# Scatter and weight transposes moved ahead of the wait for gate and up weights, in passes of four experts

## What is computed

```
gate   = weights of the top 8 of 64 experts per token        # 256 tokens in all
act    = silu(einsum('td,edf->tef', t, w_gate)) * einsum('td,edf->tef', t, w_up)
routed = einsum('tef,efd->td', act * gate[:, :, None], w_down)
```

## Time and profile before

| | |
|---|---|
| median of 3 runs | 1548.76 us (1547.97 to 1551.95) |
| profiled execution | 1552.18 us |
| its span, first to last instruction | 1550.5 us |
| TensorE busy | 1422.1 us, 92% of the span |
| transfers | 507.48 MB, mean 327 GB/s |
| mean granted clock of TensorE | 0.970 of full |

### The profile page before, as it was taken

How to read it: one execution, slowest core, us unless ns; L and a number is a source line. 1 busy time by engine, 2 the same in 40 slices (tenths; PEclk the granted TensorE clock), 3 DMA queues, 4 the chain that set the end, 5 groups by cost and what they waited for, 6 DMA issues and landing times. The chain is left out here.

```text
span 1550.5 us, 28139 instructions
## 1 busy us (share of the span) xinstructions
PE 1422.1 (92%) x11994; PEld 741.8 (48%) x11995; DVE 425.4 (27%) x1070; ACT 259.5 (17%) x485; POOL 118.0 (8%) x349
## 2 busy tenths in 40 slices
PE   3999979999999989999969998989998999999996
PEld 2675656434434434444446666564443444344442
DVE  2291774311111111111135537460111111111112
ACT  1313213211101111111113231141110111111110
POOL 2610630000000000000000026000000000000000
PEclk8899999999999999999989999989999999999999
DMA  6854950699999999999845678119999999999994
GB/s 245 281 181 174 362 193 8 284 405 421 420 419 406 410 421 404 420 418 421 359 162 174 237 267 309 52 59 405 421 421 420 421 405 410 419 413 421 414 420 189
DMA packets 114116, 507.48 MB, mean 327 GB/s; under 512 B 14880, under 2 KB 20796, under 8 KB 64572
## 3 DMA queue, kind: packets, MB, share of 16 engines
q1 hardware_dynamic: 113372, 504.43, 81.3%
q0 software_dynamic: 384, 1.05, 0.2%
q10 hardware_dynamic: 224, 0.06, 0.0%
HBM read 503.41 MB, written 2.10 MB: 326 GB/s over the span
## 5 line engine op out<-in xcount | busy, mean ns | idle before, releaser
L971 PE MATMUL ps<-ring,h 128*32 128x512 f32 x2720 | 373.3, 598 | 23.7 <-DMA ring<-in_exp_w_up 15.0
L971 PEld LDWEIGHTS ps<-ring,h 128*32 128x32 f32 x2720 | 109.5, 111 | 245.6 <-issue 245.5
L990 PE MATMUL ps<-ring,work 128*32 128x512 f32 x1360 | 199.6, 598 | 3.1 <-DVE store L1636 1.6
L971 PE MATMUL ps<-store,h 128*32 128x512 f32 x608 | 189.5, 616 | 10.8 <-issue 7.2
L997 PE MATMUL ps<-store,work 128*128 128x512 f32 x416 | 192.4, 605 | 1.6 <-DVE store L1644 1.6
L957 PEld LDWEIGHTS ps<-tm,work 128*128 128x128 bf16 x2496 | 144.4, 98 | 44.3 <-issue 43.1
L957 PE MATMUL ps<-tm,work 128*128 128x128 bf16 x2496 | 156.9, 219 | 0.3
L1634 DVE TENSOR_TENSOR work<-work,ps 128x256 f32<-128x256 f32 x52 | 21.9, 422 | 408.5 <-ACT work L1299 408.5
L997 PEld LDWEIGHTS ps<-store,work 128*128 128x128 f32 x416 | 74.7, 189 | 120.0 <-issue 116.5
L1636 DVE COPY store<-ps 128x512 f32<-128x512 f32 x52 | 36.0, 692 | 328.9 <-PE ps L990 328.9
L681 PE MATMUL ps<-ring,store 128*128 128x512 f32 (+1 forms) x256 | 100.7, 552 | 0.0
(11 more groups left out here) (296 smaller groups left out, 1222.3 us busy)
## 6 DMA issues: line engine op xcount, KB each, us to landing
ring<-in_exp_w_gate SPq DMA_DIRECT2D x102, 1024.0 KB, 14.7
ring<-in_exp_w_up SPq DMA_DIRECT2D x102, 1024.0 KB, 17.1
ring<-in_exp_w_down SPq DMA_DIRECT2D x102, 1024.0 KB, 15.4
ring<-in_w_ada SPq DMA_DIRECT2D x28, 2048.0 KB, 10.3
store<-in_exp_w_gate SPq DMA_DIRECT2D x26, 1024.0 KB, 15.2
store<-in_exp_w_up SPq DMA_DIRECT2D x26, 1024.0 KB, 17.7
work<-in_exp_w_down SPq DMA_DIRECT2D x26, 1024.0 KB, 15.4
ring<-in_w_in SPq DMA_DIRECT2D x6, 2048.0 KB, 12.5
```

The lines of the kernel that those rows point to most:

```text
L971: last = mm(ps[first:first + TILE, 4, :], X_e[:, b, kt, first:first + TILE], gate_up(slot, kt), start=(kt == 0), stop=(kt == KT - 1))
L990: last = mm(ps[first:first + TILE, 7, :], turn[:, P * j + first:P * j + first + TILE], down(slot, j, half), start=(j == 0), stop=(j == 1))
```

## The change

In a pass of four experts, other than p = 0, the two transposes of routing weights and the scatter of the rows of the pass before are issued ahead of the wait for the gate and up weights. In the other passes nothing moves. No instruction is added or removed, SyncE's, ScalarE's and VectorE's programs stay as they are.

```diff
                 used = [EXPERT_PASS.index(p) + c for c in range(len(PLACED[p]))]
+                late = p > 0 and len(used) == P // TILE
+                if late:
+                    pe.wait_ge(s["S_ready"], p + 1)
+                    turn_weights()
+                    pe.wait_ge(s["Y_kept"], 2 * p)
+                    scatter().then_inc(s["scattered"], 1)
                 for k in used:
                     pe.wait_ge(gate_in[expert_slot(k)], 32 * (k // SLOTS + 1))
                 pe.wait_ge(s["X_kept"], 2 * p + 2)
                 gate_up_pass(q, tiles(p)).then_inc(s["gu_done"], 1)
-                if p:
+                if p and not late:
                     pe.wait_ge(s["Y_kept"], 2 * p)
                     scatter().then_inc(s["scattered"], 1)
-                pe.wait_ge(s["S_ready"], p + 1)
-                turn_weights()
+                if not late:
+                    pe.wait_ge(s["S_ready"], p + 1)
+                    turn_weights()
                 pe.wait_ge(s["act_done"], p + 1)
                 turn_acts().then_inc(s["turned"], 1)
```

## The result

The changed kernel takes 1553.7 us (median of 17 runs, 1549.4 to 1560.39). The kernel before takes 1547.97 us (median of 17 runs, 1544.34 to 1552.51). The ratio is 1.0039, with a 95% interval of 1.0025 to 1.0053; the medians differ by 5.7 us. The forecast was 1556.4, slower, in a range of 1550 to 1560.

What follows compares the result with a forecast made beforehand. TensorE (92% busy) and the transfers (nine tenths in expert passes) were both taken as nearly full. Layer ends of +4.1 and +3.5 sum to 7.6, profiled 1552.18 to 1559.8; the median, 3.4 lower, gives 1556.4 us, range 1550 to 1560.

Steps and rivals of the forecast that it cites:

- the price of a pass: Each changed pass: 4.44 us added ahead of gate_up_pass, 2.68 saved behind, so it ends later by 1.76 - W.
- the clock that falls at p = 16: At p = 16, layer 2: a wait grown to 3.0 us lowers TensorE's clock, so lateness goes from +1.8 to +3.5.
- the cost of the late release: Buffers released 4.44 us late behind p = 11 leave a 2.5 us transfer hole; behind p = 20 another, 2.0.
- W: TensorE's wait ahead of a pass's gate_up_pass in the kernel before, from none at p = 11 to 3.34 us at p = 15.
- What p = 15 gains is not kept: At p = 15, layer 2: the pass ends 0.8 us sooner, but p = 16 still waits for its own weights.
- The rival in which it holds: Clock stays up at p = 16 after a 3.0 us wait; layers end +1.8 and +2.4, 1553.0 us; chance 0.12.
- the floor: Shortest time from issue to landing of up weights on a drained queue: taken as 8.9 us, with 6.8 for the range.
- the second rival: Queue always holds enough (6.8 us to landing); only last passes lose, 0.5 and 1.1 us: 1550.4 us; chance 0.16.
- called p = 6 even: At p = 6, a wait of about 1.66 us was to offset the change within 0.1 us.
- The last passes: At p = 25, the change was to lose 1.11 us in layer 1 and 0.52 in layer 2.
- the faster rival: Waits ahead of p = 25 grow long, so each last pass ends 2.68 us sooner: 1543.4 us; chance 0.07.
- Holes everywhere: Queue also runs short behind p = 1, 6 and 15, up to 2.5 us each: 1564 us; chance 0.07.

Runs made afterwards that it cites:

- after: The changed kernel, four-expert passes other than p = 0 scattering ahead, against the kernel before: 1553.7 us, ratio 1.0039; its first profile is of a 1549.4 us execution.
- after again: The changed kernel with no further edit, run and profiled a second time against the kernel before: 1554.27 against 1547.31 us, ratio 1.0042.
- before, first: First profile of the unchanged kernel before, an execution of 1552.18 us, compared pass by pass with its second profile, from a run of 1545.35 us.

## Why the prediction was right, and where it was not

The direction held, and so did the price of a pass and the clock that falls at p = 16. The time came near by luck as well: the cost of the late release was put too high, and what p = 6 does to p = 7 was left out. The time came out 2.7 us under the forecast; of that, 0.8 is that the median of before is now 1547.97 and not 1548.76. By steps, for both layers of the two profiles of after, and for the first profile of before, which shows the chance in such figures:

| | predicted | after, layers 1 and 2 | after again | before, first |
|---|---|---|---|---|
| p = 12 begins | +2.5 | +0.55, +2.2 | -0.4, +2.3 | +0.9, +0.4 |
| p = 15 ends | -0.8 | -3.1, -1.5 | -4.2, -0.5 | +1.25, 0.0 |
| p = 16 begins | +1.8 | +1.8, +2.5 | -0.3, +3.7 | +1.5, 0.0 |
| p = 16 ends | +3.5 | +3.5, +4.1 | +2.6, +6.5 | +1.5, 0.0 |
| p = 20 `gate_up_pass` begins | +5.9 | +6.5, +7.35 | +5.6, +9.7 | +1.5, +0.9 |
| p = 21 begins | +3.0 | +2.1, +2.9 | +1.2, +5.2 | +1.5, +0.8 |
| layer ends | +4.1, +3.5 | +2.7, +3.9 | +3.5, +7.9 | +1.0, +1.2 |

The ends of the two layers add up to 6.6 us in the first profile of after and to 11.4 in the second, where 7.6 was forecast and 5.7 measured between the medians. Counted from the first profile of before, from which the prediction was worked out, they make 4.4 and 9.2.

*The price of a pass, 1.76 - W: right.* Shown by p = 1 (1.82 - W) and by the run with every pass changed (2.03 for a pass without a wait). Its parts were right within 0.2 us: 0.44 + 0.44 ahead of the scatter for 0.81, and 0.96 between `gate_up_pass` and `turn_acts` for 1.17.

*What p = 15 gains is not kept: right*, shown by p = 15 alone. *The clock falls at p = 16 instead: right.* The rival in which it holds came true in one layer of two with p = 15 and 20 changed, and in one layer of two with half a scatter. In the eight layers of the whole change, all but p = 20, all but the last, and after again, it fell in each, and made `gate_up_pass` 1.4 to 2.9 us longer, where 1.7 was forecast.

*The late release: the queue runs dry, as forecast, but the size was wrong.* The term that was mis-sized is the floor: "I take 8.9". The lower bound, 6.8, was right: on a dry queue behind p = 11 and 20 the up weights landed after 6.8 to 7.5 us. The queue's reserve (landing time before, less that on a dry queue) behind p = 11 so was 3.7 to 3.9 us in the first profile of before, where the up weights landed after 10.6 and 10.8, and 4.7 to 4.9 in the second (11.9 and 11.7), and not 1.9; behind p = 20 it was 4.4 to 4.5 and not 2.9. By itself this gives the time of the second rival, 1550.4, and p = 11 alone showed what that rival said: no hole that p = 12 felt. Why gate weights took 6.7 us in the row behind pass 0, on which the 8.9 rested, and 4.9 behind p = 11 stays open.

The Trainium skill, page "DMA: Bandwidth & Descriptors", section "Latency and other measured facts", has about 0.6 us to the first byte. With two transfers of 2.5 us issued 0.4 us apart that would make a floor of some 5.2 us, an estimate from that figure. The measured floor is longer, 6.8 to 7.5 us; the first byte itself is not in any run here.

*What made up for it was not forecast: p = 6 and 7.* The prediction called p = 6 even and asked for nothing behind it. But its wait went over to p = 7, and with it the low clock, as from p = 15 to 16. Five of the kernels' profiles have p = 1, 6 and 11 changed (after, after again, all but p = 20, all but the last, all three), which makes ten layers. In eight of them the clock fell at p = 7: p = 11's `gate_up_pass` began 5.2 to 7.7 us later instead of the 4.44 forecast, the queue ran dry (up weights after 6.8 to 7.0 us), and p = 12 began 0.5 to 3.0 us later. In two the clock held at p = 7: p = 11 began 3.4 and 3.5 us later, the up weights landed after 8.0 and 8.1, and p = 12 began 0.4 and 0.2 us sooner.

p = 12 itself was late for another reason than the forecast's. It was to wait for its weights; in all eight layers it didn't wait, and the weights had landed 0.10 to 0.29 us before it began. The lateness there is TensorE's own: in layer 2 of after p = 7 ended +2.25 and p = 11 +4.28, and p = 12's old wait of 1.91 takes up only part, which leaves 2.4, where 2.2 was seen. The dry queue comes out at the same time (6.9 - 4.7 = 2.2) and so held nothing up at p = 12. It fits that p = 11 alone, and p = 1 and 6 alone, cost nothing and all three together do: p = 12's wait has room for one lateness of about 2 us, not for two. What the hole in the transfers costs further on, at p = 16, no run separates from the buffers that TensorE gave back late.

*The last passes: right in mean, with a cost that was left out.* 1.11 and 0.52 us were forecast for layers 1 and 2; where the clock held, 0.65 and 0.99 were measured. Where it fell behind the two short waits, the last pass lost 2.3 to 3.9 us. The prediction looked for low clock only behind long waits. That W grows past 1.76 in them, as the faster rival wants, was seen in one layer only (2.76, in the run of all but the last pass).

*Holes everywhere: not seen.* With p = 15 alone p = 16's weights came on time (-0.5 and -0.8), and with p = 1 and 6 alone so did p = 7's (-1.3 and -0.7).

What stays open is why the last pass alone costs as much as the whole change, and the others without it no less; its runs had the lowest mean clock, which goes part of the way. Open too is whether the clock falls in one place because it held in another: the profiles show one execution each, and the clock's places differ between executions of one kernel.

## What to carry to other kernels

Work behind a stage isn't free to move because TensorE waits ahead of it: here the scatter was the cover for ScalarE's silu and VectorE's product, and ahead of the stage it needs a copy that has just begun; leaving half of it behind kept the cover, and no loss was left that could be told from none. Where transfers set the pace, a pass that ends sooner only waits longer in the next one, and the place of the low clock moves along. A release that came later by less than the queue's reserve (landing time now, less landing time on a dry queue) left the landing where it was within 0.4 us; beyond the reserve the landing moved by the rest. So add the lateness that earlier passes bring along before you compare, and then ask when the engine itself gets there: here it came no earlier than the late weights. A wait further on takes up one lateness of its size, and not a second.

## What was not expected of the hardware

- On a dry queue in the middle of the passes 1 MB of gate weights landed 4.7 to 5.4 us after its issue, nearly as fast as a transfer alone (4.7), and the up weights issued 0.4 us later after 6.8 to 7.5.
- TensorE's clock fell from 2.4 to 1.2 GHz not only behind waits for weights, but in five of eight changed last passes also behind 0.96 and 0.77 us of waiting in the pass's end. And a wait for weights doesn't settle it: over all fourteen profiles, 18 of 43 waits of 1.95 to 3.3 us ahead of `gate_up_pass` were followed by low clock, and 32 of 36 longer ones; p = 15 kept its full clock behind 3.66 us (p = 11 alone) and 3.58 (p = 1 and 6). Of p = 16's waits of 3.6 to 5.1 us in these runs, twelve of thirteen were followed by low clock; the one that was not, was 3.99 us long:

```profile
598.93 7.07 PE L971 MATMUL ps<-ring,h 128*32 128x512 f32 x64 [3.99 <-issue]
```

- Behind waits of 3.6 and 3.8 us the clock stayed low longer (`gate_up_pass` 9.8 and 10.0 us) than behind p = 15's waits of 3.8 and 3.9 in the kernel before (8.77): the length of a wait doesn't tell how much is lost.
